# Ten of eleven up-projection tiles computed by seven block products for two tiles, with the convolution reading from SBUF

## The reference, cut to what matters

```
u = y @ w_up                       # y: 256 x 1024, w_up: 1024 x 5632
u[t] = sum_j conv_w[j] * u[t-2+j] + conv_b
gate, val = split(u, 2)
h = h + (silu(gate) * val) @ w_down   # w_down: 2816 x 1024
out = rms_norm(h, final_norm)
```

## Time and profile before

| | us |
|---|---|
| median of three runs | 1548.13 |
| lowest and highest | 1545.45, 1548.43 |
| the profiled execution | 1545.9 |
| its span | 1543.8 |
| up tiles 1 to 10 in the span | 1333.2 to 1471.4 |
| down products | 1471.4 to 1537.7 |

### The profile page before, as it was taken

One profiled execution on the slowest core, in us unless ns is written; L12 is line 12 of the kernel. 1 busy time (PEld: TensorE's weight loads), 2 busy tenths in 40 slices (PEclk: granted clock), 3 DMA queues, 4 the chain that ended last, 5 costly groups with the idle time before them and its releaser, 6 DMA issues.

```text
span 1543.8 us, 20343 instructions
## 1 busy us (share of the span) xinstructions
PE 1288.3 (83%) x8841; PEld 728.5 (47%) x8841; DVE 446.3 (29%) x911; ACT 212.2 (14%) x440; POOL 234.3 (15%) x214
## 2 busy tenths in 40 slices
PE   9999987668677679999887667758768999999998
PEld 7554433223223234865533223223224784888843
DVE  2457210001001007677311000001004446223374
ACT  1032100000000002261200000000002014211110
POOL 2414000000000006674000000000001757000000
PEclk9999999888878889999998888888889999999999
DMA  9928899999999999825799999999999981544000
GB/s 345 388 103 323 332 427 427 427 428 427 427 426 428 427 420 369 324 109 234 306 427 427 427 428 426 427 428 427 428 427 389 317 258 43 183 144 164 28 0 27
DMA packets 88279, 498.80 MB, mean 323 GB/s; under 512 B 8452, under 2 KB 31392, under 8 KB 63872
## 3 DMA queue, kind: packets, MB, share of 16 engines
q1 hardware_dynamic: 85728, 490.23, 78.3%
q0 software_dynamic: 2464, 7.29, 1.5%
HBM read 496.42 MB, written 1.07 MB: 322 GB/s over the span
## 4 chain that ended last, share of the span: by engine, by line
PE 52%; DMA 37%; DVE 6%; another core or an unknown queue 2%; issue 1%; ACT 1%; SPq 1%; DVEq 0%; POOL 0%
DMA weight_ring<-in_moe_w_down 24%; PE bank L1322 10%; PE bank L887 7%; DMA weight_ring<-in_moe_w_up 6%; PE bank L1175 6%; PE bank L884 5%; PE bank L1358 4%; PE bank L1227 4%; PE bank L1240 4%; PE bank L850 3%; DMA phase_room<-in_moe_w_down 3%; DMA phase_room<-in_moe_w_gate 3%; PE bank L1150 1%; PE bank L1094 1%
## 5 line engine op out<-in xcount | busy, mean ns | idle before, releaser
L1175 PE MATMUL bank<-weight_ring,x_tok 128*32 128x256 f32 x3328 | 226.0, 421 | 102.3 <-DMA weight_ring<-in_moe_w_up 87.3
L1175 PEld LDWEIGHTS bank<-weight_ring,x_tok 128*32 128x32 f32 x3328 | 110.8, 119 | 214.1 <-issue 86.9
L1227 PE MATMUL bank<-weight_ring,xT 128*32 128x512 f32 x864 | 138.4, 772 | 72.8 <-DMA weight_ring<-in_moe_w_down 64.8
L1322 PE MATMUL bank<-xT,weight_ring 128*128 128x256 f32 (+1 forms) x768 | 153.1, 362 | 0.3 <-ACT xT L1399 0.3
L2069 DVE TENSOR_TENSOR xT<-xT,bank 128x256 f32<-128x256 f32 x32 | 13.5, 421 | 456.8 <-PE bank L1175 456.8
L1322 PEld LDWEIGHTS bank<-xT,weight_ring 128*128 128x128 f32 x768 | 136.0, 190 | 17.1 <-issue 0.6
L1240 PE MATMUL bank<-x_tok,xT 128*128 128x512 f32 x256 | 126.7, 639 | 0.0
L679 POOL TENSOR_TENSOR weight_ring<-weight_ring 128x512 f32<-128x512 f32 x36 | 48.4, 1380 | 457.5 <-DMA weight_ring<-in_w_qkv 443.1
L688 POOL TENSOR_TENSOR weight_ring<-weight_ring 128x512 f32<-128x512 f32 x72 | 97.5, 1387 | 76.1 <-DVE weight_ring L1726 34.4
L1227 PEld LDWEIGHTS bank<-weight_ring,xT 128*32 128x32 f32 x864 | 27.4, 124 | 154.2 <-DMA weight_ring<-in_moe_w_down 73.8
L2074 DVE COPY x_tok<-bank 128x512 f32<-128x512 f32 x32 | 22.1, 692 | 254.0 <-PE bank L1227 254.0
(11 more groups left out here) (291 smaller groups left out, 1451.0 us busy)
## 6 DMA issues: line engine op xcount, KB each, us to landing
weight_ring<-in_moe_w_gate SPq DMA_DIRECT2D x52, 2048.0 KB, 49.5
weight_ring<-in_moe_w_up SPq DMA_DIRECT2D x52, 2048.0 KB, 49.6
weight_ring<-in_moe_w_down SPq DMA_DIRECT2D x52, 2048.0 KB, 49.1
phase_room<-in_moe_w_gate SPq DMA_DIRECT2D x12, 2048.0 KB, 47.8
phase_room<-in_moe_w_up SPq DMA_DIRECT2D x12, 2048.0 KB, 50.0
weight_ring<-in_w_up SPq DMA_DIRECT2D x22, 1024.0 KB, 10.4
phase_room<-in_moe_w_down SPq DMA_DIRECT2D x8, 2048.0 KB, 50.9
weight_ring<-in_gla_w_in SPq DMA_DIRECT2D x6, 2048.0 KB, 23.3
```

Source lines behind the costliest of these rows:

```text
L1175: last = mm(bank[q * CAP:(q + 1) * CAP, 0:S], xinT[:, 4 * r + k, j * CAP:(j + 1) * CAP], w[k][:, q * S:(q + 1) * S], start=(r == 0 and k = ...
L1227: last = mm(PS[i][k * CAP:(k + 1) * CAP, :], hidT[:, 4 * r + k, :], w[k][:, i * 512:(i + 1) * 512], start=(r == 0), stop=(r == 1), skip_gr ...
L1322: last = mm(PS[bank_pair + c // 2][:, at + tokens.start:at + tokens.stop], w[:, k, c * P:(c + 1) * P], xT[:, k, tokens], start=(k == 0), s ...
```

## The change

Tile 0 is made as before. Tiles 1 to 10 become five projections `UPS` (u = 9 to 13) of two tiles each, in the TURNED form: seven products of 16 matmuls with 128 tokens moving, in place of 64 matmuls with 256. The even-numbered u use banks 0 to 3, the others 4 to 7. POOL makes their first and last weight sums after those of O_ATT. The tokens' sums are made once, for all five, into `acc`. `take_value` writes the first tile of a pair into `pre[0]` (1024 columns of the room) and the second into `pre[1]` (`gain_row`). The taps and the convolution of these ten tiles read `pre`, in SBUF. The order of the convolution is 0, 2, 1, 4, 3 and so on: the second tile of a pair is whole after number 7, the first after number 9. ScalarE's taps no longer run one tile ahead of its Silu. The down projection's first product waits for `min(2i+3, 11)` gated tiles in place of `min(2i+2, 11)`.

```
+    CONV_ORDER = [0] + [i + 1 - j for i in range(1, UPT, 2) for j in range(2)]
...
-        first_weight_sums(O_ATT)
-        last_weight_sums(O_ATT)
+        for u in (O_ATT, *UPS):
+            first_weight_sums(u)
+            last_weight_sums(u)
...
-            for i in range(1, UPT):
-                n = T_UP + i
-                arrived(pe, n)
-                if i >= 3:
-                    pe.wait_ge(conv_done, i - 2)
-                up(n, 2 * (i % 3), slice(0, S)).then_inc(tile_used, 1)
+            for u in UPS:
+                for x in (1, 2, 3, 6, 5, 7, 4):
+                    if (u, x) == (UPS[0], 3):
+                        pe.wait_ge(convT_copied, 1)
+                    elif (u, x) == (UPS[1], 1):
+                        pe.wait_ge(conv_done, 1)
+                    block_product(u, x)
...
-                        pe.wait_ge(ff_ready, min(2 * i + 2, UPT))
+                        pe.wait_ge(ff_ready, min(2 * i + 3, UPT))
...
+            for s, i in enumerate(CONV_ORDER):
+                if s == 0:
+                    act.wait_ge(tile_used, T_UP + 1)
+                else:
+
+                    act.wait_ge(out_taken, 9 * UPS[(s - 1) // 2] + (7 if s % 2 else 9))
+                if s >= 2:
+                    act.wait_ge(ff_ready, s - 1)
                 for c in range(4):
                     n = 2 * i + c % 2 + FB * (c // 2)
...
                 last.then_inc(taps_done, 1)
...
+                act.wait_ge(conv_done, s + 1)
+                f(conv[:, s % 2, 0:2], conv[:, s % 2, 0:2], ACT.Silu).then_inc(ff_silu, 1)
...
+                        u = PS[c // 2][:, (c % 2) * S:(c % 2 + 1) * S - back] if s == 0 else pre[s % 2][:, c, 0:S - back]
+                        dst = conv[:, s % 2, c, back:S]
...
+            dve.wait_ge(tr_act, 3 * U_FFN + 3)
+            dve.wait_ge(tr_dve, U_FFN + 1)
+            left_and_right_sums(UPS[0])
             convolve(0)
...
+            for g, u in enumerate(UPS):
+                dve.wait_ge(conv_done, 2 * g + 1)
+                take_value(u, 1, 1, 0, 0, None)
+                gated(2 * g)
+                take_value(u, 2, 2, 0, 0)
+                second_weight_sums(u)
+                take_value(u, 3, 3, 0, 1, None)
+                middle_values(u)
+                convolve(2 * g + 1)
+                last_values(u)
+                gated(2 * g + 1)
+                convolve(2 * g + 2)
+            gated(UPT - 1)
```

More of the change, by code:

```diff
@@ L1311, in ffn @@
         def ffn():
-            def up(n, bank_pair, tokens, tile=None):
-                w = slot(n).rearrange("p (k n) -> p k n", k=KC)
+            turn_only(acc, U_FFN, 0)
+            arrived(pe, T_UP)
+            w = slot(T_UP).rearrange("p (k n) -> p k n", k=KC)
+            for tt in range(TT):
                 for c in range(4):
-                    at = (c % 2) * S
-                    if (tile, c) == (0, 3):
+                    at = (c % 2) * S + tt * P
+                    if (tt, c) == (0, 3):
                         turn_only(acc, U_FFN, 1)
                     for k in range(KC):
[L1320 to L1323, removed]
+                        if c == 0 and k % 4 == 0:
+                            turned_bank(U_FFN, 2 * tt + k // 4)
+                        last = mm(PS[c // 2][:, at:at + P], w[:, k, c * P:(c + 1) * P], xT[:, k, tt * P:(tt + 1) * P],
                                   start=(k == 0), stop=(k == KC - 1), skip_group_check=True)
[L1325 to L1331, removed]
             last.then_inc(tile_used, 1)
@@ L1365, in ffn @@
             pe.wait_ge(left_ready, 3)
+            pe.wait_ge(out_taken, 9 * (UPS[-1] + 1))
             product(3, left_sum(4), 1, 1, 4)
@@ L2167, in ffn, with convolve @@
             dve.wait_ge(convT_copied, 1)
-            def convolve(i):
-                dve.wait_ge(taps_done, i + 1)
+            def convolve(s):
+                i = CONV_ORDER[s]
+                dve.wait_ge(taps_done, s + 1)
                 for back in (1, 2):
@@ L2180, in convolve, with gated @@
                 last.then_inc(conv_done, 1)
-            convolve(0)
-            for i in range(UPT):
-                if i + 1 < UPT:
-                    convolve(i + 1)
-                dve.wait_ge(ff_silu, i + 1)
-                dve.wait_ge(conv_done, i + 1)
-                v.tensor_tensor(ffh[:, 2 * i:2 * i + 2, :], conv[:, i % 2, 0:2], conv[:, i % 2, 2:4], ALU.mult
-                                ).then_inc(ff_ready, 1)
+            def gated(s):
+                i = CONV_ORDER[s]
+                dve.wait_ge(ff_silu, s + 1)
+                dve.wait_ge(conv_done, s + 1)
+                v.tensor_tensor(ffh[:, 2 * i:2 * i + 2, :], conv[:, s % 2, 0:2], conv[:, s % 2, 2:4], ALU.mult
+                                ).then_inc(ff_ready, 1)
+            dve.wait_ge(tr_act, 3 * U_FFN + 3)
+            dve.wait_ge(tr_dve, U_FFN + 1)
+            left_and_right_sums(UPS[0])
+            convolve(0)
+            for g, u in enumerate(UPS):
[11 more added lines that the diff above has]
+            gated(UPT - 1)
             dve.wait_ge(ff_ready, UPT)
```

36 lines of the change are left out of this document (15 added, 21 removed).

## The result

The changed kernel takes 1549.57 us, the kernel before 1547.79 in the same session: a ratio of 1.0016 [1.001, 1.0023], or 2.5 us more. (These two are medians; the ratio is that of the means, 1549.84 to 1547.34.) One of the 20 executions of the changed kernel took 1837.26 us at a mean granted clock of 0.647 and is left out of the ratio. The point of the prediction was 3.8 us more, and the range held the result. The 13.1 us that the seven products save are there, and all of them and 2.5 more are given back in waits and in the steps that these waits pace.

What follows compares the result with a forecast made beforehand. TensorE's work per tile was taken to set the end; 125.1 + 1.3 + 4 x (2.25 + 0.8) + 3.4 = 142.0 us against 138.2, +3.8, gave 1551.9 us on the median, range 1546 to 1559.

Steps and rivals of the forecast that it cites:

- the lower bound of the chain: Whole kernel: with no port wait and taps at 1.93 us, the change gives +0.2 us.
- Seven products: TensorE in the up pairs: 25.02 us a pair; five cost 125.1 in place of 138.2, 13.1 us gross gain.
- Lateness in pairs 2 to 5 with the port: VectorE's sums before product 6: 2.9 us late, costing TensorE 2.25 a pair, plus 0.8 for the port.
- The slack of 0.63: Product 6 of a turned pair: TensorE loses the lateness of VectorE's sums less 0.63 us.
- The port: Second tile's convolution overlaps POOL's SBUF instructions by 2.1 us: 0.8 us lost in each of four pairs, bounds 0 and 1.9.
- The tail: First down product, step 4: TensorE waits for the last gated tile, 3.4 us lost.
- First pair: First up pair: VectorE's sums start at 1343.2, due 1341.24, so 1.96 us late and 1.3 lost.
- POOL hides: POOL's weight sums in the up pairs: 16.3 us of 25 a pair, hidden; they may delay the tokens' norm without cost.
- Cheap convolution: Rival, VectorE's convolution from SBUF: 2.1 us in place of 3.34, 9.8 us less in all, 1538; chance 0.2, 0.13 faster.
- The clock: Rival, TensorE's granted clock falls after four stalls and the tail: 2 us each, +10 more, 1562; chance 0.1.
- The whole convolution at the port: Rival, POOL one instruction later in each pair: 3 us in place of 0.8, 9 above the forecast, 1561; chance 0.1.
- Doesn't do what it says: Rival, up pairs: no fewer matmul columns; excluded by the loops, 112 x 128 against 64 x 256 for each pair.

Runs made afterwards that it cites:

- The filled tail: Changed kernel with down products 1 and 2 both taking their first four steps before either takes its last two: 1546.36 us, ratio 0.9996 to the kernel before.
- another order: Changed kernel with VectorE's second weight sums ahead of number 2 and the gate's multiplication: 1547.06 us, ratio 0.9996; repeated, 1547.62 us, ratio 1.0.
- the added instruction: Changed kernel with one more 512-column VectorE instruction, result unused, ahead of the sums of pairs 2 to 5: 1553.41 us, ratio 1.0041 to the kernel before.

## Why the prediction was right

**Outcome.** Forecast +3.8 us, measured +2.5 (1.5 to 3.6 by the interval). The mechanisms were the ones named, and all terms but one were within 0.3 us. That one, the first pair, carries 1.2 of the 1.3 us between them. It also decides the side: the prediction gave 0.52 to a loss above 3.1 us and 0.35 to one too small to tell, and 2.5 us is among the latter. One sum of it is off: by its own items the lower bound of the chain is -0.1 us (3.8 less 3.2 for the port and 0.7 for ten sets of taps), not +0.2.

- *Seven products*, 25.02 us a pair: measured 25.11 in the first pair, which has no wait. The 0.1 stands in its products 1 and 2 (7.25 us from 1335.56 to 1342.81, against 7.15); the products behind them take 3.573 each. Right.
- *Lateness in pairs 2 to 5 with the port*, 2.25 + 0.8 = 3.05 each: measured 28.00 - 25.02 = 2.98. The chain was put at 14.5 + 0.8 = 15.3 us from the end of product 7, measured 15.18; taps were 2.08 for 2.0 and the SBUF convolution 3.37 for 3.34. The slack of 0.63 held: in the changed kernel 3.57 us of lateness (step 0 of product 3 ends at 1368.71, the sums begin at 1372.28) cost 2.98.
- *The port*, 0.8: measured 0.76, but for half of the overlap that was reckoned, at twice the price. I had product 7's end at 23.7 us of the pair, from the loss without the port; with it the end is 24.43, and the overlap 0.98 us in place of 2.1. The two errors cancel. That this term came out is luck: a price of 0.8 for a whole 2.1 us would have been too low by half.
- *The tail*, 3.4: the wait is 3.34, and the two products take 3.60 more than in the kernel before. Nothing is gained or lost behind it. The filled tail took it all back, 3.57.
- *First pair*, 1.3: measured 0.1, and none of it a wait for the sums. **This step failed**: "Silu loads its table now with nothing ahead of it, 1.28 + 0.64". The load doesn't stand behind the convolution; ScalarE ran it right after the taps, ahead of the wait that belongs to the Silu. Without its 1.28, and with three short instructions that start 0.61 to 0.66 us apart where I put 0.7 and more, the sums were 0.37 us late, not 1.96, which the slack of 0.63 takes up. With the load forced behind the wait the pair was 1.15 longer. The Trainium skill (ScalarE: Activation LUTs, Step-by-step: what each stage is for) says that the load stands as an instruction right before its activation; the trace agrees, and shows that the wait stands between the two.
- *POOL hides*: it does; the first sums of the first pair ran at 1314.38, under the output projection. They did hold up the norm of the tokens, one VectorE instruction of 1.28 us taking 2.37 beside them, and the way to the first pair was no longer by it (41.4 us in both).

**The rivals.** *Cheap convolution*: out, the SBUF form takes 3.37 us. The Trainium skill's fixed cycles (VectorE: DVE Perf Modes, the TRN2 errata) hold for ScalarE in sign and about in size: 0.15 us on four taps, where an estimate from the page's cycles is 0.17. The 0.5 us off VectorE's convolution, estimated in the same way, were not there (3.37 from SBUF, 3.33 from PSUM). *The clock*: not in the changed kernel, but the mechanism is real. It cost 2.8 us in the tail of another order, and it fell inside pairs where TensorE waited longer: in two of four late pairs with the added instruction (2.15 us waits, 0.42 us each), in three of four and two of four with POOL held back. That is less than the 2 us a stall of the prediction. *The whole convolution at the port*: no, but POOL held back by one wait made it happen, at 2.1 us. *Doesn't do what it says*: TensorE has 480 more records than in the earlier trace rows, two for each of 5 x (112 - 64) = 240 more matmuls. My "560 more" was their whole number, 5 x 112, and not what they are above the 320 of before; no term of the sum rested on it.

## What to carry to other kernels

A faster form for the busiest engine is worth what the others leave of it: here 13.1 us of saved matmuls stood behind a serial chain of taps, convolution, taps, convolution on two idle-looking engines (busy 19.3 and 5.4 us of 28). Walk that chain from the last value it needs to the first wait it ends, and group what waits for the same partner, so that one crossing serves two tiles: that order and the two interleaved down products turned +2.5 us into -11 (by the stage).

## What the runs showed of the hardware

- The table load ran ahead of the semaphore wait of its activation: 1.28 us at 1337.97, with 2.79 us of waiting behind it. One small activation between the wait and the Silu put the load on the path, 1.15 us.
- Between a VectorE instruction stream with two SBUF inputs and POOL's sums both lose: eight instructions of 255 columns 3.37 to 5.48 us, POOL's four 4.97 to 5.77, at an overlap of 3.1 us.
- The granted clock after 3.35 us of idle TensorE at the same place was 0.50 in two profiles of one order and 1.00 in two of another. Of three waits of 2.15 us in one profile, two were followed by 0.50 and one by 1.00, at the same work before and behind them.
